# A chain of eight layers on one core: signs turned, forget rows as matmuls, whole first units, a new table of modulation sums

## The chip, the cores and the metric

The kernel runs on one core of a Trainium2 chip. The metric is the device time of one execution in microseconds (us), lower is better. It is one program for the whole chain.

## The reference

Eight stages follow one another on x of 256 x 1024 (float32): moba attention with pooling, a gated feed-forward with a causal convolution (conv), and then twice a plain ffn, an attention mixer and a second plain ffn; the mixer is swa (window 128, sinks, relative bias) the first time and fox (forget gates) the second.

```python
mod = c_act @ ada_w[l] + ada_b[l]              # shift, scale, gate of every stage
h = rms_norm(x, norm1_g[l]) * (1 + scale1) + shift1
...
def swiglu(h, w13, w2):
    gate, up = jnp.split(h @ w13, 2, axis=-1)
    return (jax.nn.silu(gate) * up) @ w2
...
# swa: m = max(max(s), sink); p = exp(s - m); denom = sum(p) + exp(sink - m)
s = jnp.einsum('bqhgd,bkhd->bhgqk', qb, kb).astype(jnp.float32) + bias
...
# fox: F is the running sum of log_sigmoid(fl + b_f)
s = jnp.einsum('bqhd,bkhd->bhqk', qb, k).astype(jnp.float32)
s = s + Fq[..., None] - F[:, :, None, :]
p = jax.nn.softmax(s, axis=-1)
...
x = x + 0.5 * mod[:, 0, 2][:, None, :] * swiglu(h, ffn_w13[layer, 0], ffn_w2[layer, 0])
```

## The kernel before

**Units of weights.** All weights stream once through SBUF in 215 units of 2048 columns on 128 partitions. SyncE loads a unit into `raw` (a ring of five); ACT copies it to `hi` in a rounded format (line 487); DVE writes `lo` = raw − hi (line 915, in `split_to`). PE then multiplies with three matmuls for each product: hi·hi, hi·lo and lo·hi (`product`). The next raw load into a slot of the ring waits for `unit_done` of the unit five earlier. The stages are moba (units 0 to 23), conv (24 to 56), ffn (57 to 89), swa (90 to 99), ffn (100 to 132), ffn (133 to 165), fox (166 to 181) and ffn (182 to 214); in what follows they are stages 0 to 7, and a unit is counted from its stage's start.

**An ffn stage.** Eleven slices j of 256 hidden columns. Units (j, 0) and (j, 1) hold the slice's gate and up weights, each for half of the contraction; both are multiplied for tile 0 and then for tile 1 of the tokens. Unit (j, 2) holds the down weights. From slice 2 on the order is (j, 0), (j, 1), (j−1, 2): units 3j−1, 3j, 3j+1. On ACT, in `ffn_step`, stand the hi split of unit 3j+1, the silu of tile 0, the silu of tile 1 (line 580), which waits for `unit_done` of unit 3j, and behind it the hi split of unit 3j+2. On DVE the lo split of unit 3j+1, the two products of silu and up (line 998), the lo split of unit 3j+2, and the low part of the hidden (line 1008) stand in this order, with the pieces and columns that go with each lo split.

**Modulation.** The vector of shifts, scales and gates is computed in chunks of 512 outputs, six a stage. The weights of a chunk come in four pieces over POOL's queue. DVE multiplies a piece by c and adds it to `ada_sum` (`pieces`, lines 874 and 877); the first piece of chunk c waits for `ada_used`, the sum of chunk c−2. PE adds up over the partitions with four matmuls of one column (`sums`, line 1392), and waits there for the columns of all chunks before (`mod_ready`). DVE adds the bias and writes the column (`columns`, line 899). `gate_rows` (line 1404) turns a stage's gate columns to rows on PE, into the same bank M as the sums; it waits until the columns of all sums issued so far are written, and the next user of M waits for ACT's copy (`gate_copy`, line 546). The dictionaries `PIECES_AT`, `SUMS_AT`, `COLS_AT`, `GATES_AT`, computed at the head of the file, say at which unit each of these stands: on PE a sum or a gate turn comes ahead of the unit's matmuls (`take`); on DVE pieces and then columns come behind the unit's lo split. `CHUNKS_IN` says how many chunks fall in a stage. By the table before, stage 2 (nine chunks) has sums at units 7, 10, 13, 16, 19 and so on, columns at 9, 12, 15, 18 and gate turns at 13 and 16; stages 4 and 5 (eight chunks) have sums at 7, 10, 14, 17, 21, columns at 9, 12, 16, 19 and gate turns at 13 and 17.

**Start of a stage.** x is normalised on ACT (line 515), transposed on PE (`turn_x`, line 1412), scaled out of the banks on ACT (line 527), and split on DVE into `h_hi` and `h_lo` (lines 950 and 952), for two tiles of 128 tokens, in halves. In stages 0 and 1 `first_units` (line 1321 and on) runs units 0 and 1 for tile 0 alone with 128-column matmuls, and then for tile 1.

**Attention.** A head's logits are two matmuls (lines 1609 and 1610); DVE adds the bias and takes the maximum (lines 1081 and 1082), negates it (1085), in swa adds the sink (1089); ACT exponentiates (657, 658); PE transposes and multiplies by V. In fox DVE first forms the bias of the head from the forget rows in TB, Fq and the mask (1071 and 1073), and POOL fetches these rows: it writes them to DRAM (456) and reads them to all partitions (459). The steps t = 0 to 19 overlap the heads, and carry the remaining rows of the in-projection (`step_rows`), lo splits, pieces and out pieces (`step_out`); at the end of the steps stand out pieces (3,0), (1,1), (2,1), the transposes of the next stage's tile 0 and (3,1).

## Time and profile before

| | before |
|---|---|
| times of three runs, us | 1655.14, 3947.6, 1659.46 (the median) |
| profiled execution, us | 1657.64 |
| its span, us | 1655.8 |
| mean granted TensorE clock | 0.933 |
| PE busy, us (share) | 1518.7 (92%) |
| DVE busy | 1075.1 (65%) |
| ACT busy | 725.3 (44%) |
| POOL busy | 135.4 (8%) |
| DMA, mean | 203 GB/s |

The span is that of the profiled execution from its first to its last instruction; times in the rows are microseconds from its start. PE is the TensorE matmul queue, PEld its weight loads. A granted clock of 1.00 is 2.4 GHz and 0.50 is 1.2 GHz. A row of a timeline gives start, duration, engine, line, operation, what is written from what, and in brackets the idle time of the engine before it and what ended that.

### The profile page before, as it was taken

What the parts mean: (1) busy time and instruction counts of PE and PEld (TensorE: products, weight loads), DVE (VectorE), ACT (ScalarE), POOL (GpSimd) and SP (SyncE); (2) the same over time, 40 slices, a digit from 0 to 9 for tenths busy, and PEclk for the clock granted to TensorE, in tenths of its full rate; (3) what the DMA queues carried; (4) which work ended last, traced back from release to release, by engine and by line L of the source; (5) the groups of instructions that cost most, each with busy time, mean ns of one, the idle gap of its engine ahead of it and who ended that gap; (6) DMA issues with size and microseconds to landing.
All of it is one profiled execution on the core that took longest, in us unless ns stands there. A gap on an engine that the chain in (4) does not pass through costs nothing.

```text
span 1655.8 us, 19732 instructions
## 1 busy us (share of the span) xinstructions
PE 1518.7 (92%) x7897; PEld 1282.6 (77%) x7897; DVE 1075.1 (65%) x1571; ACT 725.3 (44%) x1030; POOL 135.4 (8%) x195
## 2 busy tenths in 40 slices
PE   1898898999998999998799999999999987999998
PEld 1897897988887777886467888878888765678886
DVE  4226776478787666775856767677676467666454
ACT  3224443444446433354546334553445555563442
POOL 1000110010110111100100111001110000000000
PEclk9569899799999999999689999999999897899999
DMA  9325676377684887863417888678886354067562
GB/s 320 116 90 175 201 247 204 115 228 242 216 260 135 263 270 241 294 224 143 140 52 224 291 278 274 206 227 290 273 270 210 126 204 152 26 204 237 174 196 80
DMA packets 194990, 335.97 MB, mean 203 GB/s; under 512 B 8338, under 2 KB 138030, under 8 KB 194772
## 3 DMA queue, kind: packets, MB, share of 16 engines
q1 hardware_dynamic: 167536, 236.02, 42.3%
q0 software_dynamic: 26784, 98.47, 18.7%
q8 instruction: 63, 1.03, 0.3%
q10 hardware_dynamic: 580, 0.23, 0.1%
q14 instruction: 27, 0.22, 0.0%
HBM read 333.58 MB, written 1.10 MB: 202 GB/s over the span
## 4 chain that ended last, share of the span: by engine, by line
PE 73%; DVE 12%; ACT 7%; issue 4%; DMA 3%; SPq 0%; ACTq 0%; DVEq 0%
PE bank L1461 9%; PE bank L1463 9%; PE bank L1462 9%; PE bank L1424 7%; PE bank L1426 6%; PE bank L1425 6%; PE bank L1321 5%; PE bank L1322 5%; PE bank L1323 5%; DVE lo L915 3%; ACT hi L487 3%; DVE ada_sum L877 3%; PE bank L1392 2%; PE bank L1472 1%; DMA ada<-in_ada_w 1%
## 5 line engine op out<-in xcount | busy, mean ns | idle before, releaser
L915 DVE TENSOR_TENSOR lo<-raw,hi 128x2048 fp32r<-128x2048 f32 x215 | 490.9, 2287 | 102.2 <-ACT hi L487 101.7
L487 ACT ACTIVATE hi<-raw 128x2048 fp32r<-128x2048 f32 x215 | 405.4, 1909 | 32.6 <-DMA raw<-in_w_out 19.3
L1461 PE MATMUL bank<-hi,h_hi 128*128 128x512 f32 x704 | 277.6, 394 | 2.6 <-DVE lo L915 1.8
L1463 PE MATMUL bank<-hi,h_lo 128*128 128x512 f32 x704 | 274.4, 390 | 0.0
L1462 PE MATMUL bank<-lo,h_hi 128*128 128x512 f32 x704 | 274.1, 389 | 0.0
L877 DVE SCALAR_TENSOR_TENSOR ada_sum<-ada,c_act,ada_sum 128x512 f32<-128x512 f32 x308 | 231.1, 750 | 34.4 <-DMA ada<-in_ada_w 26.4
L1424 PE MATMUL bank<-hi,o_hi 128*128 128x512 f32 x504 | 209.4, 415 | 18.5 <-DVE lo L915 16.4
L449 POOL DMA_DIRECT2D ada<-in_ada_w x176 | 125.5, 713 | 1230.4 <-DVE ada_sum L877 1202.6
L1321 PE MATMUL bank<-h_hi,hi 128*128 128x256 f32 (+1 forms) x640 | 196.7, 307 | 17.1 <-DVE lo L915 10.9
L1426 PE MATMUL bank<-hi,o_lo 128*128 128x512 f32 x504 | 202.1, 401 | 0.0
L1425 PE MATMUL bank<-lo,o_hi 128*128 128x512 f32 x504 | 201.5, 400 | 0.0
L1322 PE MATMUL bank<-h_lo,hi 128*128 128x256 f32 (+1 forms) x640 | 194.1, 303 | 0.0
L1323 PE MATMUL bank<-h_hi,lo 128*128 128x256 f32 (+1 forms) x640 | 194.1, 303 | 0.0
L580 ACT ACTIVATE KT<-bank 128x256 f32<-128x256 f32 x88 | 33.8, 384 | 324.4 <-PE bank L1463 323.9
L1461 PEld LDWEIGHTS bank<-hi,h_hi 128*128 128x128 f32 x704 | 132.2, 188 | 32.5 <-DVE lo L915 3.5
L1463 PEld LDWEIGHTS bank<-hi,h_lo 128*128 128x128 f32 x704 | 132.2, 188 | 28.3
L1321 PEld LDWEIGHTS bank<-h_hi,hi 128*128 128x128 f32 x640 | 137.2, 214 | 20.2 <-issue 15.7
L1462 PEld LDWEIGHTS bank<-lo,h_hi 128*128 128x128 f32 x704 | 132.3, 188 | 26.4
L1322 PEld LDWEIGHTS bank<-h_lo,hi 128*128 128x128 f32 x640 | 137.2, 214 | 0.0
L1323 PEld LDWEIGHTS bank<-h_hi,lo 128*128 128x128 f32 x640 | 137.0, 214 | 0.0
L1424 PEld LDWEIGHTS bank<-hi,o_hi 128*128 128x128 f32 x504 | 97.9, 194 | 41.3 <-DVE lo L915 20.7
L998 DVE TENSOR_TENSOR KT<-KT,bank 128x256 f32<-128x256 f32 x88 | 36.5, 420 | 125.8 <-ACT KT L580 125.8
(209 smaller groups left out, 1884.3 us busy)
## 6 DMA issues: line engine op xcount, KB each, us to landing
ada<-in_ada_w POOLq DMA_DIRECT2D x176, 512.0 KB, 4.9
raw<-in_ffn_w SPq DMA_DIRECT2D x176, 512.0 KB, 5.2
raw<-in_ffn_w SPq DMA_DIRECT2D x44, 1024.0 KB, 6.0
raw<-in_w_up SPq DMA_DIRECT2D x22, 1024.0 KB, 5.1
raw<-in_w_in SPq DMA_DIRECT2D x16, 1024.0 KB, 6.9
raw<-in_fox_w_in SPq DMA_DIRECT2D x12, 1024.0 KB, 5.2
raw<-in_w_down SPq DMA_DIRECT2D x11, 1024.0 KB, 5.3
raw<-in_swa_w_in SPq DMA_DIRECT2D x6, 1024.0 KB, 5.2
```

Of the source, the lines that this page charges most:

```text
L487: nc.scalar.activation(hi[:, n % NS, :], raw[:, n % NS, :], ACT.Copy).then_inc(hi_ready, 1)
L877: nc.vector.scalar_tensor_tensor(acc, in0=src, scalar=c_act[:, col:col + 1], in1=acc, op0=ALU.mult, op1=ALU.add).then_inc(ada_step, 1)
L915: nc.vector.tensor_tensor(lo[:, n % NS, :], raw[:, n % NS, :], hi[:, n % NS, :].bitcast(F32), ALU.subtract).then_inc(lo_ready, 1)
L1321: mm(outp, wh, xh, start=start, stop=False, skip_group_check=True)
L1322: mm(outp, wh, xl, start=False, stop=False, skip_group_check=True)
L1323: return mm(outp, wl, xh, start=False, stop=stop, skip_group_check=True)
L1424: mm(outp, xk_hi, wh[:, k, cut], start=start, stop=False, skip_group_check=True)
L1425: mm(outp, xk_hi, wl[:, k, cut], start=False, stop=False, skip_group_check=True)
L1426: ins = mm(outp, xk_lo, wh[:, k, cut], start=False, stop=stop, skip_group_check=True)
L1461: mm(bank[:, :], xk_hi, wh[:, i, :], start=k == 0, stop=False, skip_group_check=True)
L1462: mm(bank[:, :], xk_hi, wl[:, i, :], start=False, stop=False, skip_group_check=True)
L1463: ins = mm(bank[:, :], xk_lo, wh[:, i, :], start=False, stop=k == KD - 1, skip_group_check=True)
```

## The change

Seven things change together. (1) Stages 0 and 1 run their first two units whole, on both tiles with 256-column matmuls (`whole_units`); in conv the transposes of tile 1 stand ahead of them. (2) `CHUNKS_IN` gives stages 4 and 5 nine chunks and fox none, and the table puts a sum two units later where a gate turn stands at its unit, its column two units behind it: stages 2, 4 and 5 have sums at 7, 10, 15, 18, 19, 22, 25, 28, 31, columns at 9, 12, 17, 20, 21, 24 and gate turns at 13 and 16. (3) Logits are kept negated: DVE writes the negative minimum directly, and the two small operations (1085, 1089) go; the exponential takes a scale of −1. (4) In fox the forget terms become two extra matmuls of K = 2 for each head; TB is filled with ones on POOL, two rows a head are written by four small transfers, and lines 1071 and 1073, the copy of Fq and its transposes go. (5) The in-projection in fox uses three banks in turn, and more of its rows come ahead of the steps in swa (12 instead of 8 of 16 of the last two blocks) and fewer in fox. (6) Out pieces (1,1) and (2,1) stand in steps 15 and 18. (7) In swa two pieces stand ahead of the steps, and eight in them; block roots, evictions and splits of ACT and DVE are placed in other steps.

```diff
-ROWS_STEP = {"swa": 2, "fox": 6}
-ROWS_LEFT = {"swa": 8, "fox": 40}
+ROWS_FROM = {"swa": 12, "fox": 16}
+ROWS_STEP = {"swa": 2, "fox": 7}
...
-CHUNKS_IN = [6, 6, 9, 3, 8, 8, 2, 2]
+CHUNKS_IN = [6, 6, 9, 3, 9, 9, 0, 2]
...
-        for c0 in range(n0):
-            SUMS_AT[w0 + at[4 * c0 + 3] + 2] = 1
-            COLS_AT[w0 + min(at[4 * c0 + 3] + 4, 32)] = 1
-        free = [u0 for u0 in range(at[7] + 5, 33) if not any(0 < u0 - at[4 * c0 + 3] - 2 <= 2 for c0 in range(n0))]
-        GATES_AT[w0 + free[0]] = (s0, 0)
-        GATES_AT[w0 + next(u0 for u0 in free if u0 >= free[0] + 2)] = (s0, 1)
+        due = [at[4 * c0 + 3] + 2 for c0 in range(n0)]
+        free = [u0 for u0 in range(at[7] + 5, 33) if not any(0 < u0 - u1 <= 2 for u1 in due)]
+        turns = (free[0], next(u0 for u0 in free if u0 >= free[0] + 2))
+        GATES_AT[w0 + turns[0]], GATES_AT[w0 + turns[1]] = (s0, 0), (s0, 1)
+        for u1 in due:
+            u1 += 2 * (u1 in turns)
+            SUMS_AT[w0 + u1] = 1
+            COLS_AT[w0 + min(u1 + 2, 32)] = 1
...
-PIECES_STEP = {"moba": (), "swa": range(0, 10), "fox": range(2, 8)}
-SUMS_STEP = {"moba": (), "swa": (2, 6, 10), "fox": (4, 8)}
-COLS_STEP = {"moba": (), "swa": (3, 7, 10), "fox": (5, 9)}
+PIECES_STEP = {"moba": (), "swa": range(0, 8), "fox": ()}
+SUMS_STEP = {"moba": (), "swa": (1, 5, 9), "fox": ()}
+COLS_STEP = {"moba": (), "swa": (2, 6, 10), "fox": ()}
...
+                pool.wait_ge(am_done, HEAD0[6])
+                nc.gpsimd.memset(TB[0:66, :, :], 1.0).then_inc(rows_ones, 1)
+                pool.wait_ge(rows_ones, 1)
                 pool.wait_ge(nft_ready, 1)
-                pool.dma_start(scratch_f[:, :], nFT).then_inc(forget_out, 16)
+                pool.dma_start(scratch_f.rearrange("n h t -> h n t"), F_rows).then_inc(forget_out, 16)
                 pool.wait_ge(forget_out, 16)
...
-                pool.dma_start(TB[:, :, :].rearrange("p a b -> p (a b)"), src).then_inc(bias_in, 16)
-            last_before_forget = PIECES * sum(CHUNKS_IN[:6]) + 1
+                for odd in range(2):
+                    for n in range(2):
+                        pool.dma_start(TB[64 * odd + 1 - n:64 * odd + 2 - n, 8 - 8 * n:16 - 8 * n, :],
+                                       scratch_f[n:n + 1, odd:16:2, :]).then_inc(bias_in, 16)
...
-                nc.scalar.activation(pr[:, 0:P], pr[:, 0:P], ACT.Exp, bias=st[:, 2:3], accum_out=st[:, 4:5])
-                ins = nc.scalar.activation(pr[:, P:384], pr[:, P:384], ACT.Exp, bias=st[:, 3:4], accum_out=st[:, 5:6])
+                nc.scalar.activation(pr[:, 0:P], pr[:, 0:P], ACT.Exp, bias=st[:, 2:3], scale=-1.0, accum_out=st[:, 4:5])
+                ins = nc.scalar.activation(pr[:, P:384], pr[:, P:384], ACT.Exp, bias=st[:, 3:4], scale=-1.0,
+                                           accum_out=st[:, 5:6])
                 if KINDS[s] == "swa":
-                    ins = nc.scalar.activation(st[:, 6:8], st[:, 6:8], ACT.Exp)
+                    ins = nc.scalar.activation(st[:, 6:8], st[:, 2:4], ACT.Exp, bias=sink[:, h:h + 1])
...
-                b0, b1 = TB[:, h, P:2 * P], TB[:, h, :]
-                if kind == "fox":
...
-                    nc.vector.scalar_tensor_tensor(f0, in0=TB[:, h, 0:P], scalar=Fq[:, 0, h:h + 1], in1=mask[:, P:2 * P],
-                                                   op0=ALU.add, op1=ALU.add)
-                    nc.vector.scalar_tensor_tensor(f1, in0=TB[:, h, :], scalar=Fq[:, 1, h:h + 1], in1=mask,
-                                                   op0=ALU.add, op1=ALU.add).then_inc(bias_ready, 1)
-                    b0, b1 = f0, f1
-                    dve.wait_ge(bias_ready, h + 1)
...
+                b0, b1 = (mask[:, P:2 * P], mask) if kind == "fox" else (TB[:, h, P:2 * P], TB[:, h, :])
+                most = nsink[:, h:h + 1] if kind == "swa" else -LOWEST
                 dve.wait_ge(qk_done, n + 1)
                 if n >= 3:
                     dve.wait_ge(tr_done, n - 2)
-                nc.vector.tensor_tensor_reduce(pr[:, 0:P], L[:, 0:P], b0, 1.0, least, ALU.add, ALU.max, st[:, 0:1])
-                nc.vector.tensor_tensor_reduce(pr[:, P:384], L[:, P:384], b1, 1.0, least, ALU.add, ALU.max,
-                                               st[:, 1:2]).then_inc(max_done, 1)
-                dve.wait_ge(max_done, n + 1)
-                ins = nc.vector.tensor_scalar(st[:, 2:4], st[:, 0:2], -1.0, None, ALU.mult)
-                if kind == "swa":
-                    ins.then_inc(neg_done, 1)
-                    dve.wait_ge(neg_done, h + 1)
-                    ins = nc.vector.tensor_scalar(st[:, 6:8], st[:, 2:4], sink[:, h:h + 1], None, ALU.add)
-                ins.then_inc(am_done, 1)
+                nc.vector.tensor_tensor_reduce(pr[:, 0:P], L[:, 0:P], b0, -1.0, most, ALU.add, ALU.min, st[:, 2:3])
+                nc.vector.tensor_tensor_reduce(pr[:, P:384], L[:, P:384], b1, -1.0, most, ALU.add, ALU.min,
+                                               st[:, 3:4]).then_inc(am_done, 1)
...
+                    pieces(2)
...
-                        if t in (0, 4):
-                            block_sums(s, 4 + t // 4)
-                            block_norm(s, 4 + t // 4)
-                        if t in (1, 3, 5, 7, 9):
-                            split_through(s, 6 + (t - 1) // 2)
+                        if t in (0, 3):
+                            block_sums(s, 4 + t // 3)
+                            block_norm(s, 4 + t // 3)
+                        if t in (2, 4, 6, 8, 10):
+                            split_through(s, 6 + (t - 2) // 2)
...
+                    dve.wait_ge(cum_done, 1)
+                    nc.vector.tensor_copy(F_rows[:, 0, :], A[1][0:16, 0:T])
+                    nc.vector.tensor_scalar(F_rows[:, 1, :], A[1][0:16, 0:T], -1.0, None, ALU.mult).then_inc(nft_ready, 1)
...
-            def first_units(s):
-                for t in range(2):
-                    for u in range(2):
-                        w, bank = W0[s] + u, G[u]
-                        if t == 0:
-                            take(w)
-                        wh, wl = unit_of(w, KD)
+            def whole_units(s):
+                if s:
+                    turn_x(s, 1)
+                for u in range(2):
+                    w, bank = W0[s] + u, G[u]
+                    take(w)
+                    wh, wl = unit_of(w, KD)
+                    for n in range(2):
                         for k in range(KD):
-                            pe.wait_ge(h_ready, 4 * s + 2 * t + k // 4 + 1)
-                            xk_hi, xk_lo = h_hi[:, k, P * t:P * (t + 1)], h_lo[:, k, P * t:P * (t + 1)]
...
-                            for n in range(2):
-                                ins = product(bank[:, T * n + P * t:T * n + P * (t + 1)], wh[:, k, P * n:P * (n + 1)],
-                                              wl[:, k, P * n:P * (n + 1)], xk_hi, xk_lo, k == 0 and n == 0, k == KD - 1)
-                        if t:
-                            ins.then_inc(unit_done, 1)
-                    if t == 0 and s:
-                        turn_x(s, 1)
+                            if u == 0 and n == 0:
+                                pe.wait_ge(h_ready, 4 * s + 3 + k // 4)
+                            ins = product(bank[:, T * n:T * (n + 1)], wh[:, k, P * n:P * (n + 1)],
+                                          wl[:, k, P * n:P * (n + 1)], h_hi[:, k, :], h_lo[:, k, :], k == 0, k == KD - 1)
+                    ins.then_inc(unit_done, 1)
...
+                if KINDS[s] != "fox":
+                    mm(L[:, 0:P], q[:, 0:P], k[:, 0:P], start=True, stop=True)
+                    mm(L[:, P:384], q[:, P:T], k, start=True, stop=True).then_inc(qk_done, 1)
+                    return
+                f_q, f_k = TB[row:row + 2, 8 + h // 2, :], TB[row:row + 2, h // 2, :]
+                mm(L[:, 0:P], q[:, 0:P], k[:, 0:P], start=True, stop=False, skip_group_check=True)
+                mm(L[:, 0:P], f_q[:, 0:P], f_k[:, 0:P], start=False, stop=True, skip_group_check=True)
+                mm(L[:, P:384], q[:, P:T], k, start=False, stop=False, skip_group_check=True)
+                mm(L[:, P:384], f_q[:, P:T], f_k, start=False, stop=True, skip_group_check=True).then_inc(qk_done, 1)
...
                     elif t == 14:
                         step_out(s, 0, 1)
+                    elif t == 15:
+                        step_out(s, 1, 1)
                     elif t == 17:
                         step_out(s, 2, 0)
                     if t >= 3:
                         values(s, t - 3)
+                    if t == 18:
+                        step_out(s, 2, 1)
                 step_out(s, 3, 0)
-                step_out(s, 1, 1)
-                step_out(s, 2, 1)
                 turn_x(s + 1, 0)
...
-                    block_rows(s, 3, 0, 0, KD)
-                    pe.wait_ge(nft_ready, 1)
-                    steps(s, (1, 3, 4, 6))
+                    pe.wait_ge(bias_in, 96)
+                    steps(s, (3, 4, 5, 6))
```

**Order 1.** DVE in stage 2, from the last piece behind unit 15's lo split on. Line 915 is the lo split of unit 16, then of unit 17; 877 are pieces, 899 is a column. Before:

```order
L877 SCALAR_TENSOR_TENSOR ada_sum<-ada,c_act,ada_sum 128x512 [waits ada_step]
L899 TENSOR_TENSOR modc<-bank,cols 128x4 [waits ada_used]
L915 TENSOR_TENSOR lo<-raw,hi 128x2048 [waits hi_ready]
L877 SCALAR_TENSOR_TENSOR ada_sum<-ada,c_act,ada_sum 128x512 [waits ada_step,ada_full0]
L877 SCALAR_TENSOR_TENSOR ada_sum<-ada,c_act,ada_sum 128x512 [waits ada_step]
L998 TENSOR_TENSOR KT<-KT,bank 128x256 [waits silu_ready] x2
L915 TENSOR_TENSOR lo<-raw,hi 128x2048 [waits hi_ready]
```

After, the same splits are line 923, the pieces 885, the column 907:

```order
L885 SCALAR_TENSOR_TENSOR ada_sum<-ada,c_act,ada_sum 128x512 [waits ada_step]
L923 TENSOR_TENSOR lo<-raw,hi 128x2048 [waits hi_ready]
L885 SCALAR_TENSOR_TENSOR ada_sum<-ada,c_act,ada_sum 128x512 [waits ada_step,ada_full0]
L885 SCALAR_TENSOR_TENSOR ada_sum<-ada,c_act,ada_sum 128x512 [waits ada_step]
L1006 TENSOR_TENSOR KT<-KT,bank 128x256 [waits silu_ready] x2
L923 TENSOR_TENSOR lo<-raw,hi 128x2048 [waits hi_ready]
L885 SCALAR_TENSOR_TENSOR ada_sum<-ada,c_act,ada_sum 128x512 [waits ada_step,ada_full1]
L885 SCALAR_TENSOR_TENSOR ada_sum<-ada,c_act,ada_sum 128x512 [waits ada_step]
L907 TENSOR_TENSOR modc<-bank,cols 128x4 [waits ada_used]
L1016 TENSOR_TENSOR o_lo<-bank,o_hi 128x512 [waits hid_hi_done]
```

The column of the last sum moved from ahead of unit 16's lo split to behind unit 17's lo split and its piece.

**Order 2.** PE in stage 2, at the end of unit 15 (slice 5, second half). Before, both the gate turn (line 1404) and the sum (line 1392) stand ahead of unit 16's first matmul (line 1424):

```order
L1462 MATMUL bank5<-lo,h_hi 128x512
L1463 MATMUL bank5<-hi,h_lo 128x512
L1404 MATMUL bank6<-kon,modc 128x128 [waits gate_ready,mod_ready]
L1404 MATMUL bank6<-kon,modc 128x128 x3
L1392 MATMUL bank6<-ones,ada_sum 128x1 [waits gate_ready,mod_ready,ada_step]
L1392 MATMUL bank6<-ones,ada_sum 128x1 x3
L1424 MATMUL bank0<-hi,o_hi 128x512 [waits hid_ready,lo_ready]
```

After, the sum (line 1371) stands ahead of unit 15's first matmul:

```order
L1440 MATMUL bank5<-hi,h_hi 128x512
L1441 MATMUL bank5<-lo,h_hi 128x512
L1442 MATMUL bank5<-hi,h_lo 128x512
L1371 MATMUL bank6<-ones,ada_sum 128x1 [waits gate_ready,mod_ready,ada_step]
L1371 MATMUL bank6<-ones,ada_sum 128x1 x3
L1440 MATMUL bank4<-hi,h_hi 128x512 [waits lo_ready]
```

And at the end of unit 15 the gate turn (line 1383) stands alone ahead of unit 16:

```order
L1441 MATMUL bank5<-lo,h_hi 128x512
L1442 MATMUL bank5<-hi,h_lo 128x512
L1383 MATMUL bank6<-kon,modc 128x128 [waits gate_ready,mod_ready]
L1383 MATMUL bank6<-kon,modc 128x128 x3
L1403 MATMUL bank0<-hi,o_hi 128x512 [waits hid_ready,lo_ready]
```

The gate turn now follows a sum that was issued one unit before it, and the next sum (line 1371) stands ahead of unit 18.

**Order 3.** PE in fox, the first logits. Before:

```order
L1575 MATMUL bank5<-lo,h_hi 128x512
L1576 MATMUL bank5<-hi,h_lo 128x512
L1609 MATMUL bank0<-KT,QT 128x128 [waits am_done,bk_ready]
L1610 MATMUL bank0<-KT,QT 128x256
L1609 MATMUL bank1<-KT,QT 128x128 [waits am_done]
```

After, with the forget matmuls from TB (lines 1599 and 1601):

```order
L1558 MATMUL bank6<-hi,h_lo 128x512
L1598 MATMUL bank0<-KT,QT 128x128 [waits am_done,bk_ready]
L1599 MATMUL bank0<-TB 128x128
L1600 MATMUL bank0<-KT,QT 128x256
L1601 MATMUL bank0<-TB 128x256
L1598 MATMUL bank1<-KT,QT 128x128 [waits am_done]
```

Each head has four matmuls where it had two.

## Rows read from the trace of the kernel before

**Rows 1.** Cores: span and mean granted clock

```profile
core 0: 1655.8 us, clock 0.933
```

**Rows 2.** Windows, core 0 (engines' busy us, PEclk, DMA share, GB/s): stages 2, 4; swa's, fox's steps

```profile
525.00:737.30 212.30, 204.56 (x939) 168.59 (x937) 150.50 (x167) 90.63 (x103) 25.65 (x36) 0.97 0.76 251
872.00:1073.90 201.90, 197.40 (x932) 163.01 (x931) 144.19 (x158) 90.78 (x103) 22.81 (x32) 1.00 0.77 255
...
780.20:835.20 55.00, 39.88 (x145) 25.99 (x146) 47.68 (x134) 29.69 (x74) 7.12 (x10) 0.67 0.42 130
1345.80:1413.20 67.40, 56.73 (x230) 40.45 (x230) 47.92 (x130) 38.15 (x75) 4.28 (x6) 0.82 0.41 136
```

**Rows 3.** Windows of first units: stage 0 (two), conv (two), and 256-column matmuls in conv

```profile
63.00:104.00 41.00, 41.00 (x193) 41.00 (x193) 7.79 (x9) 9.04 (x13) 0.00 (x0) 0.50 0.12 38
104.20:109.00 4.80, 4.80 (x24) 4.80 (x24) 2.36 (x2) 2.56 (x3) 0.00 (x0) 0.50 0.72 219
291.60:302.20 10.60, 10.60 (x97) 10.60 (x97) 9.37 (x11) 6.78 (x10) 0.14 (x1) 1.00 0.40 137
305.70:325.90 20.20, 20.20 (x100) 20.20 (x101) 2.77 (x6) 3.68 (x7) 0.00 (x0) 0.53 0.17 53
423.10:434.50 11.40, 11.40 (x97) 11.40 (x97) 8.07 (x10) 3.38 (x4) 1.43 (x2) 1.00 0.72 239
```

**Rows 4.** Timeline of DVE, stage 0, tile 1's first half

```profile
64.95 0.69 DVE L952 TENSOR_TENSOR h_lo<-tn,h_hi 128x512 fp32r<-128x512 f32 x1
```

**Rows 5.** Windows where PE's clock has fallen and comes back

```profile
264.60:269.40 4.80, 4.77 (x15) 4.19 (x16) 4.38 (x2) 2.40 (x2) 2.56 (x3) 0.50 0.54 167
512.00:515.00 3.00, 2.99 (x7) 2.41 (x8) 2.97 (x4) 2.77 (x3) 0.00 (x0) 0.50 0.00 0
515.00:518.00 3.00, 3.00 (x14) 2.40 (x14) 1.64 (x2) 0.00 (x0) 0.00 (x0) 0.97 0.00 0
```

**Rows 6.** Timeline of ACT, conv's start: tile 1's scaling

```profile
298.16 1.32 ACT L515 ACTIVATE work<-x,rms 128x512 f32<-128x512 f32 x2
```

**Rows 7.** Timeline of ACT, stage 5, behind unit 15

```profile
1177.10 0.38 ACT L580 ACTIVATE KT<-bank 128x256 f32<-128x256 f32 x1 [2.34 <-PE bank L1463]
```

**Rows 8.** Timeline of DVE, stage 5, unit 17's split and piece

```profile
1179.33 2.29 DVE L915 TENSOR_TENSOR lo<-raw,hi 128x2048 fp32r<-128x2048 f32 x1 [1.39 <-ACT hi L487]
1181.54 1.53 DVE L877 SCALAR_TENSOR_TENSOR ada_sum<-ada,c_act,ada_sum 128x512 f32<-128x512 f32 x2
```

**Rows 9.** Timeline of PE, stage 2, the sum at unit 13

```profile
611.90 1.02 PE L1392 MATMUL bank<-ones,ada_sum 128*128 128x1 f32 x8 [1.96 <-ACT gate L546]
```

**Rows 10.** Timeline of DVE in swa's steps

```profile
808.04 0.17 DVE L1085 TENSOR_SCALAR stat<-stat 128x2 f32<-128x2 f32 x1
808.24 0.23 DVE L1089 TENSOR_SCALAR stat<-stat,sink 128x2 f32<-128x2 f32 x1
...
811.79 2.29 DVE L915 TENSOR_TENSOR lo<-raw,hi 128x2048 fp32r<-128x2048 f32 x1 [0.70 <-ACT hi L487]
```

**Rows 11.** Timeline of ACT in swa's steps, a table load and the next exponential

```profile
806.32 1.28 ACT L657 ACT_TABLE_LOAD   x1
808.51 0.40 ACT L657 ACTIVATE work<-work,stat 128x128 f32<-128x128 f32 x1 [0.90 <-DVE stat L1089]
```

**Rows 12.** Timeline of PE, swa's end, the start of out piece (3,0)

```profile
863.36 0.47 PE L1424 MATMUL bank<-hi,o_hi 128*128 128x512 f32 x1 [1.07 <-DVE o_lo L1107]
```

**Rows 13.** Timeline of ACT, swa's end: tile 0 normalised for the next stage

```profile
869.16 1.34 ACT L515 ACTIVATE work<-x,rms 128x512 f32<-128x512 f32 x2 [0.23 <-DVE rms L943]
```

**Rows 14.** Timeline of DVE in fox, the first bias

```profile
1344.15 0.35 DVE L1071 SCALAR_TENSOR_TENSOR tn<-TB,Fq,kon 128x128 f32<-128x128 f32 x1 [3.16 <-DMA TB<-forget_rows]
```

**Rows 15.** Groups of PE by shape, whole span: the logits

```profile
L1610 PE MATMUL bank<-KT,QT 64*128 64x256 f32 x80 | 26.4, 436 | 0.0
L1609 PE MATMUL bank<-KT,QT 64*128 64x128 f32 x80 | 20.7, 361 | 18.8 <-DVE stat L1085 6.6 <-DVE stat L1089 5.9 <-issue 2.9
```

**Rows 16.** Timeline of POOL in fox: the broadcast of the forget rows

```profile
1335.30 0.58 POOL L459 DMA_DIRECT2D TB<-forget_rows  x1 [4.28 <-DMA forget_rows<-tn]
```

More of the change, by code:

```diff
@@ L265, in bank_of, with product_bank @@
             return (G[0], G[1], A[2], A[3])[u % 4] if u in QK_UNITS[KINDS[s]] else G[u % 2]
-        def product_bank(b, t):
-            return A[2 + b] if t and b < 2 else G[b] if b < 2 else G[t]
+        def product_bank(s, b, t):
+            if b < 2:
+                return A[2 + b] if t else G[b]
+            return (G[0], G[1], M)[(2 * (b - 2) + t) % 3] if KINDS[s] == "fox" else G[t]
         def logit_bank(h):
@@ L473, in _ @@
             by_distance(1, 16)
+            load_pieces(6)
+            forget_rows()
             load_pieces(NST)
@@ L1591, in step_rows @@
             def step_rows(s, t):
[L1593 to L1596 removed]
+                kind = KINDS[s]
+                first = ROWS_FROM[kind] + ROWS_STEP[kind] * t
+                for r in range(first, min(first + ROWS_STEP[kind], 2 * KD * (len(BLOCKS[kind]) - 2))):
+                    n = r // KD
+                    block_rows(s, 2 + n // 2, n % 2, r % KD, r % KD + 1)
             def logits(s, h):
```

169 lines of the change are left out of this document (72 added, 97 removed).

## The prediction

> **What bounds the kernel now.** First the span and the clock: 1655.8 us at a mean granted TensorE clock of 0.933 [rows 1]. Then the windows by stage [rows 2]: in a plain ffn stage PE is busy 197.4 of 201.9 us at clock 1.00, with DVE at 144 and ACT at 91. There every idle microsecond of PE is a microsecond of the end. In the swa steps it is otherwise: of 55.0 us DVE is busy 47.7 and PE 39.9 at 0.67, so DVE sets the pace. The windows of the first units [rows 3] show PE fully busy but at clock 0.50 and on 128-column matmuls, which are dear by the column. So I price PE in ffn stages by waits, in the steps by DVE's work, and in the first units by count and clock.
>
> **Whole first units, stage 0.** Before, 192 matmuls of 128 columns take 41 us at 0.50, 0.213 each [rows 3], and end at about 104.2. They begin as soon as tile 0 is split. Now 96 matmuls of 256 columns begin when tile 1's first h_lo is there: 64.95 + 0.69 = 65.6 [rows 4]. The same form at half clock takes 4.80/24 = 0.20 each, and on the full clock 11.40/97 = 0.118 [rows 3]. If all stay at half clock it is 19.2 us, to 84.9, a gain of 19. If the clock comes back after some 5 us, as it does elsewhere [rows 5], it is 24 × 0.20 + 72 × 0.12 = 13.4, to 79.1, a gain of 25. I take −25, since steady work got the clock back within 5 us where the stretches show it return [rows 5]; bound −19, and 0 by a rival below. The chain to unit 2's splits has been idle long before, so nothing new is late.
>
> **Whole first units, conv.** Before, tile 0's half (97 matmuls, 10.6 us at 1.00) ran under tile 1's normalising, and tile 1's half took 20.2 us at 0.53, to 325.9 [rows 3]. Now nothing runs until tile 1 is there: its scaling on ACT ends at 299.5 [rows 6], then transposes, the four scalings out of the banks, a cast and an h_lo of 0.69, with pieces between on DVE: about 303.0. With 13.4 us behind it, 316.4, a gain of 9.5. At half clock throughout (19.2), 322.2, a gain of 3.7. Clock 0.53 in the old second half says that idle costs it here too; I keep the 13.4. One sum moved away from a gate turn at unit 17 is 0.8 more.
>
> The isolated back-to-back gap that the Trainium skill ("TensorE: Matmul & The Clock Gate", section "Back-to-back issue gap") gives, N/1.2 cold and N/2.4 + 2.5 ns warm, prices by columns. By it, whole units save nothing, and only the later start would be left. The rows speak against it: 97 matmuls of half the width took 10.6 us and 97 of the full width 11.4, both at 1.00 [rows 3]; the same section says that the formula under-counts for small N.
>
> **The table of sums, columns and gates in ffn stages.** This is the largest term. Stages 2, 4 and 5 now have nine chunks each, with sums at units 15, 18, 19 and gate turns at 13 and 16. A gate turn (gate_rows) waits for the columns (mod_ready) of all sums issued so far. At unit 16 that includes the sum of unit 15, whose column DVE now writes only behind the lo split of unit 17 and its piece. Likewise the sum at unit 19 waits for the column of unit 18's sum, which stands behind lo of unit 20. PE executes in order, so everything of unit 16 is queued behind that wait. And lo(17) cannot be early: its hi on ACT stands behind the silu of tile 1, and that waits for unit 15's last matmul. From stage 5: the silu starts at 1177.10 when PE's last matmul releases it [rows 7]; hi follows it on ACT and releases lo at 1179.33; lo runs to 1181.6 and the piece to 1183.07 [rows 8]; the column adds some 0.15. PE was done at about 1176.9. The wait is 6.3 us; a blocked piece on DVE (chunk c waits for the sum of c−2) adds up to 0.9. I take 6.8 a wait, six waits: 40.8 (38 to 43). The clock then falls: behind an idle the rows show 3 to 5 us at 0.50 before 0.97 [rows 5], so half of that, 1.5 to 2.4, is lost; 2.0 × 6 = 12. Against it, stage 2 already pays for nine chunks and for two collisions of sum and gate (1.96 us for the copy of the gate [rows 9]): 212.3 against 201.9 of stage 4 [rows 2], less 0.8 for its additional sum, leaves 9.6 that go. Stages 4 and 5 lose 0.8 each by one more sum and win 0.8 each by a gate and a sum that no longer meet. Four more pieces each on DVE are 3.1 us, under PE. Sum: 40.8 + 12 − 9.6 = +43.2 (37 to 55).
>
> **Swa.** DVE sets the pace. The two small stat operations (0.17 and 0.23 [rows 10], with gaps about 0.42) leave each head; ten heads in the pace-setting part give −4.2. Two pieces of 1.53 leave the steps [rows 8]: −3.1. The waits of lo for hi, 0.70 [rows 10], go in five steps, since ACT's hi is now a step ahead: −3.5. The block root in step 0 adds two table loads of 1.28 on ACT [rows 11]: +2.6. Together −8.2. The Trainium skill ("ScalarE: Activation LUTs", section "What ACT_TABLE_LOAD costs") adds a drain of about 1.38 us to each switch; by it the −8.2 would be −5.4. The load ends at 807.60, and the exponential behind it starts at 808.51 after 0.90 idle that DVE ended [rows 11], so a drain does not show, though it could lie in that idle. At the tail: two out pieces of 12 matmuls, half a unit each (a unit is 197.4/33 = 6.0 with its small matmuls [rows 2], 5.6 without, so 5.6 for both), ran behind piece (3,0) and covered tile 0's normalising. Moved to t = 15 and 18 they meet few gaps: 1.07 before (3,0) [rows 12] and one half as long, 1.6. So (3,0) starts 4.0 later. Normalised rows are there at 869.16 + 1.34 = 870.5 [rows 13], 7.1 behind the start of (3,0), where before the transposes came 8.3 behind: −1.2, up to −1.8. PE idles in between, clock +1.5. Tail +4. Swa: −4 (−9 to +2).
>
> **Fox.** Per head two DVE operations (the first 0.35 [rows 14]) become two K = 2 matmuls on PE. The forms nearest by shape take 0.361 and 0.436 [rows 15], 0.88 a head with a gap: 16 × 0.88 = +14 on PE. Seven block rows move from ahead of the steps into them: 7 × 3 matmuls at 0.23 = +4.8. The two sums there go: −1.6. Together 17.2 more work in the steps, in which PE waits 67.4 − 56.7 = 10.7 us at a clock of 0.82 [rows 2]: the waits take 10.7 of it, and a denser PE gets back perhaps 4 of the clock. That leaves +2.5. The start: before, POOL issued the broadcast of 2 MB at 1335.3 [rows 16], and DVE had it at 1344.15 after waiting 3.16 [rows 14]. Now four small transfers land by about 1335, and PE, with fewer rows ahead of the steps, idles some 5.6 for them, then starts the logits at about 1341, 1.3 earlier than before. The moved out pieces and a thinner cover at the end cost 4, as in swa. Total +5; if the waits take all and the clock recovers −5, if they take half +14.
>
> **Sum.** −25 − 10.3 + 43.2 − 4 + 5 = +8.9 on the profiled execution's own 1657.6 us: 1666.5. That execution lies between the other two usable times, 1655.1 and 1659.5 (the median), so I do not shift it: **1666**. About 2% is what a measurement of this kernel can tell from no change, 1626 and 1693.
>
> **Rivals.**
> *The columns come in time.* If the six waits don't show (DVE or ACT ahead of what stage 5's rows show, or my reading of the table is off by a chunk), the ffn term is −9.6 and the result about 1614. For it: only the order shows the wait. Against: the waits name the very semaphores, and silu, hi and lo stand in that order [rows 7, 8].
> *The clock stays at half between the waits.* The waits at 16 and 19 are three units apart: 3/33 of 197.4 us [rows 2], 17.2 without the small matmuls, at full clock. If the clock doesn't come back there, this stretch becomes 34, three times: +51, less 3 × 2.0 already counted: about 1712, slower. It decides where a wait costs more than 6.4 us of clock in place of 2.0. For: 41 us of busy 128-column work stayed at 0.50 [rows 3]. Against: 512-column work got back to 0.97 within 3 us [rows 5].
> *Whole units give nothing*, because PE's time goes by columns: stage 0 then ends 2.7 later by its later start, conv 1 earlier (303.0 + 10.6 + 11.4), 36 above the forecast: 1703, slower. For: in stage 0 PE shows no idle at all. Against: 0.213 a matmul of 128 columns and 0.20 of 256 at the same half clock [rows 3].
> *Fox waits longer*: the fill of TB and five small transfers arrive as late as the old broadcast, and the K = 2 matmuls find no gaps: fox +20, about 1681.
>
> **How the numbers follow.** Forecast 0.70 (its own range 1643 to 1691), columns in time 0.13, clock at half 0.07, whole units nothing 0.02, fox longer 0.08. The range leaves out the first and the third rival: 1638 to 1694. Faster is the first rival and a tail, 0.14; slower the second and third and a tail, 0.11; the rest 0.75.
>
> **What would show it.** In the changed profile: stage 0's first units end near 79 to 85; in stages 2, 4 and 5 the gate matmul at unit 16 and the sum at unit 19 each show an idle of 6 to 7 us released by DVE's column, and each stage takes 215 to 222 us; swa's steps are shorter by about 8 us, its tail longer; fox's first logits near 1341 less the shift. Idles of under 2 us at these two places would make the forecast wrong by 40 us; a granted clock of 0.50 across whole units between them would make it too low.

## The result

| | before | after |
|---|---|---|
| median, us (18 runs each) | 1656.82 | 1668.51 |
| profiled execution's span, us | 1655.8 | 1669.1 |
| mean granted clock | 0.933 | 0.945 |

The ratio of after to before is 1.0064, with a 95% interval of 1.0048 to 1.008: slower by 0.6%, clear of noise and well inside 2%. One run of each kernel took over twice as long and is no part of the ratio. The prediction was 1666, in a range of 1638 to 1694.

The change in time by stage, each counted from the first transposes for it (their weight load) to those for the next, from the two traces:

| stage | before | after | difference | forecast |
|---|---|---|---|---|
| 0, moba | 287.7 | 261.0 | −26.7 | −25 |
| 1, conv | 236.6 | 225.9 | −10.7 | −10.3 |
| 2, 4, 5, ffn | 618.8 | 662.8 | +44.0 | +43.2 |
| 3, swa | 134.4 | 133.6 | −0.8 | −4 |
| 6, fox | 175.5 | 180.6 | +5.1 | +5 |
| 7, ffn | 203.0 | 205.3 | +2.3 | 0 |

So a kernel that moved by 12 us holds a gain of 37 and a loss of 44. The windows of after by stage (ffn 2, 4 and 5; columns as in [rows 2]):

```profile
486.90:706.60 219.70, 203.38 (x942) 167.75 (x941) 149.63 (x167) 90.76 (x103) 25.65 (x36) 0.96 0.74 244
...
840.10:1061.00 220.90, 205.44 (x939) 170.17 (x940) 151.31 (x168) 91.37 (x104) 25.66 (x36) 0.95 0.71 234
1061.00:1283.20 222.20, 205.66 (x941) 169.37 (x941) 150.54 (x170) 90.75 (x103) 27.78 (x35) 0.95 0.72 237
```

In stage 4, PE is now idle for 15 us where it was idle for 4.5, with the clock at 0.95 in place of 1.00: both a wait and what the wait does to the clock.

The timeline of PE in stage 2 of after, at the gate turn of unit 16 and the sum of unit 19:

```profile
594.87 2.08 PE L1383 MATMUL bank<-kon,modc 128*128 128x128 f32 x8 [6.18 <-DVE modc L907]
...
621.50 1.84 PE L1371 MATMUL bank<-ones,ada_sum 128*128 128x1 f32 x8 [6.32 <-DVE ada_sum L885]
```

The six such waits in the three stages are 6.18, 6.32, 6.12, 6.21, 6.12 and 6.59 us, 37.5 together. The rows of DVE ahead of the first of them tell why:

```profile
583.19 0.49 DVE L882 TENSOR_SCALAR ada_sum<-ada,c_act 128x512 f32<-128x512 f32 x1 [4.33 <-PE bank L1371]
...
591.01 2.28 DVE L923 TENSOR_TENSOR lo<-raw,hi 128x2048 fp32r<-128x2048 f32 x1
593.21 1.53 DVE L885 SCALAR_TENSOR_TENSOR ada_sum<-ada,c_act,ada_sum 128x512 f32<-128x512 f32 x2
594.66 0.15 DVE L907 TENSOR_TENSOR modc<-bank,cols 128x4 f32<-128x4 f32 x1
```

The column (line 907) stands behind the lo split of unit 17 (the row at 591.01) and its pieces; it ends at 594.81, and the gate matmul starts at 594.87. The row of the second wait names a piece (line 885) as its releaser, but a column of the same kind ended at 621.40 and PE's weight load began at 621.48, so there too it is the column. The first row is a piece that was held up: DVE waited 4.33 us for the sum that the table had moved.

The first units, after (windows; stage 0 from 70.2 on, and conv), answer to [rows 3]:

```profile
70.20:79.10 8.90, 8.90 (x69) 8.90 (x69) 2.33 (x2) 2.40 (x2) 0.00 (x0) 1.00 0.34 105
276.40:290.00 13.60, 13.60 (x100) 13.60 (x101) 2.70 (x6) 3.12 (x5) 0.00 (x0) 0.86 0.38 117
```

Of stage 0's 96 whole matmuls the first starts at 65.93 and the last at 80.09, where before the first units ended near 104. In conv the first starts 15.3 us behind the stage's start and the last 28.5; the forecast had 15.3 and 28.7 for start and end.

### The profile page after: what moved, and what is told of

It reads as the page before. It is cut to its first block, busy times and chain, and to the rows that moved or that the text cites. A ratio compares the mean times of both kernels' runs of the same rounds, so it can differ in the third digit from the quotient of the medians.

```text
span 1669.1 us, 19395 instructions
## 1 busy us (share of the span) xinstructions
PE 1507.7 (90%) x7767; PEld 1256.2 (75%) x7767; DVE 1054.2 (63%) x1484; ACT 733.3 (44%) x1034; POOL 140.5 (8%) x199
## 4 chain that ended last, share of the span: by engine, by line
PE 75%; DVE 13%; ACT 5%; DMA 4%; issue 3%; SPq 0%; ACTq 0%; POOL 0%; DVEq 0%; POOLq 0%
PE bank L1440 8%; PE bank L1442 8%; PE bank L1441 8%; PE bank L1403 7%; PE bank L1404 6%; PE bank L1405 6%; PE bank L1307 4%; PE bank L1309 4%; PE bank L1308 4%; DVE lo L923 4%; DVE ada_sum L885 4%; DMA ada<-in_ada_w 3%; PE bank L1371 2%; ACT hi L493 2%; PE bank L1556 2%
## 5 line engine op out<-in xcount | busy, mean ns | idle before, releaser
L1403 PE MATMUL bank<-hi,o_hi 128*128 128x512 f32 x504 | 213.8, 424 | 16.4 <-DVE lo L923 16.4
L1307 PE MATMUL bank<-h_hi,hi 128*128 128x256 f32 x576 | 167.7, 291 | 19.3 <-DVE lo L923 10.6
L1308 PE MATMUL bank<-h_lo,hi 128*128 128x256 f32 x576 | 165.0, 287 | 0.0
L1309 PE MATMUL bank<-h_hi,lo 128*128 128x256 f32 x576 | 164.9, 286 | 0.0
L1403 PEld LDWEIGHTS bank<-hi,o_hi 128*128 128x128 f32 x504 | 100.2, 199 | 39.5 <-DVE lo L923 20.7
L1307 PEld LDWEIGHTS bank<-h_hi,hi 128*128 128x128 f32 x576 | 112.8, 196 | 22.6 <-issue 20.1
L1405 PEld LDWEIGHTS bank<-hi,o_lo 128*128 128x128 f32 x504 | 99.4, 197 | 22.9
L1404 PEld LDWEIGHTS bank<-lo,o_hi 128*128 128x128 f32 x504 | 100.0, 198 | 18.5
L1308 PEld LDWEIGHTS bank<-h_lo,hi 128*128 128x128 f32 x576 | 112.9, 196 | 0.0
```

What stands on the lines that cost most here:

```text
L1307: mm(outp, wh, xh, start=start, stop=False, skip_group_check=True)
L1308: mm(outp, wh, xl, start=False, stop=False, skip_group_check=True)
L1309: return mm(outp, wl, xh, start=False, stop=stop, skip_group_check=True)
L1403: mm(outp, xk_hi, wh[:, k, cut], start=start, stop=False, skip_group_check=True)
L1404: mm(outp, xk_hi, wl[:, k, cut], start=False, stop=False, skip_group_check=True)
L1405: ins = mm(outp, xk_lo, wh[:, k, cut], start=False, stop=stop, skip_group_check=True)
```

## The experiments

All are compared with the kernel before on the same chip. Stage times are from each run's trace.

**The column one unit sooner.** The changed kernel with

```diff
+            moved = u1 in turns
-            u1 += 2 * (u1 in turns)
+            u1 += 2 * moved
             SUMS_AT[w0 + u1] = 1
-            COLS_AT[w0 + min(u1 + 2, 32)] = 1
+            COLS_AT[w0 + min(u1 + 2 - (moved and kind0 == "ffn"), 32)] = 1
```

> The changed kernel with one edit: in plain ffn stages the column of a moved sum stands one unit behind the sum, not two (units 16 and 19 in place of 17 and 20). My theory (PE waits at units 16 and 19 for a column that stands behind a late lo split): all six waits of 6.1 to 6.6 us go, and the clock lost behind them, so stages 2, 4 and 5 fall from about 221 to 203 to 206 us each, in all 45 to 50 us less than the changed kernel, some 1620 us. Rival (the stages are longer because nine chunks of pieces load DVE and DMA more): the waits move to the next sum or to lo splits, and at least half of the 44 us stays, above 1640 us.

Median 1630.9, ratio to before 0.9871 (0.9818 to 0.9925); the profiled span is 1622.3. Stages 2, 4 and 5 took 209.6, 208.4 and 208.1 where after has 219.7, 220.9 and 222.2: 36.7 of the 44 are gone. They did not reach the 203 to 206 of my theory, since the waits did not vanish but shrank to between 1.84 and 2.02. The rival, the load of nine chunks, had at least half of the 44 staying; 7.3 stayed. What was left needed a cause. The timelines of PE and, ahead of it, DVE in stage 2 of this run:

```profile
588.13 1.80 PE L1384 MATMUL bank<-kon,modc 128*128 128x128 f32 x8 [1.89 <-DVE modc L908]
```

```profile
580.75 0.49 DVE L883 TENSOR_SCALAR ada_sum<-ada,c_act 128x512 f32<-128x512 f32 x1 [4.33 <-PE bank L1372]
...
586.46 1.54 DVE L886 SCALAR_TENSOR_TENSOR ada_sum<-ada,c_act,ada_sum 128x512 f32<-128x512 f32 x2 [0.60 <-DMA ada<-in_ada_w]
587.92 0.15 DVE L908 TENSOR_TENSOR modc<-bank,cols 128x4 f32<-128x4 f32 x1
```

The piece waits 4.33 us for the sum of two chunks before, which stands two units later than its pieces allow. All that follows on DVE, the column too, is late by that.

**One of the two.** The same edit for the first moved sum alone (column at unit 16, the other still at unit 20):

```diff
+            moved = u1 in turns
+            first = moved and u1 == turns[0]
-            u1 += 2 * (u1 in turns)
+            u1 += 2 * moved
...
-            COLS_AT[w0 + min(u1 + 2, 32)] = 1
+            COLS_AT[w0 + min(u1 + 2 - (first and kind0 == "ffn"), 32)] = 1
```

> The changed kernel with the earlier column for the first moved sum alone (column at unit 16; that of unit 18's sum stays at unit 20). My theory, with each wait costing itself and about 2 us of clock: the wait at unit 16 goes, the one at 19 stays, half of the gain of the earlier columns, 22 to 25 us less than the changed kernel, some 1645 us. Rival (the clock is lost once for both waits, since they are three units apart): the one wait left costs over 8.5 us a stage and the gain is less than 19 us, above 1650 us.

Median 1647.75, ratio 0.9958 (0.9934 to 0.9981), span 1645.8. The trace shows the waits at unit 16 at 1.70 to 1.94 and those at unit 19 still at 6.17 to 6.26. The three stages took 216.7, 214.2 and 217.2, together 648.1: between 662.8 with both long waits and 626.1 with both shortened. One kind gave 14.7 and the other 22.0, of which 12.9 and 12.7 are idle time (three times 4.3); the rest, 1.8 and 9.3, is clock. By the ratios the steps are 18 and then 14 us. This does not decide between theory and rival. The median lies below the rival's 1650, but a gain of 14.7 by stages, or 18 by ratios, lies below the rival's 19 and short of my 22 to 25. Each kind of wait costs clock of its own (the granted clock of the three stages is 0.95 to 0.96 in after, 0.97 here and 0.98 to 0.99 with both columns early), but not the same 2 us: the second kind costs more.

**The old rule for sums beside gate turns**, nine chunks kept:

```diff
-            u1 += 2 * (u1 in turns)
+            u1 += 2 * (u1 in turns and kind0 == "conv")
```

> The changed kernel with the old rule in plain ffn stages: sums at units 13 and 16 beside the gate turns, nine chunks kept. My theory: two waits of about 2 us for the copy of the gate in each of three stages in place of 6.3, so each of these stages takes what stage 2 of the kernel before took, about 212 to 213 us; 24 us less than the changed kernel, some 1645 us. Rival (a wait costs no clock when it is only 2 us long): 208 to 209 us a stage, some 1632 us.

Median 1630.9, ratio 0.9843 (0.9793 to 0.9894), span 1637.7. The stages took 211.3, 211.0 and 210.5, in each two waits of 1.96 for the gate's copy, as in [rows 9]. By the traces that is 30 us less than after (37 by the ratios); a stage lies between my 212.5 and the rival's 208.5, and the median is nearer to the rival's 1632 than to my 1645. Its "no clock" does not hold all the same: the three stages take 632.8, against 607.5 with the table of the run "gate turns between the sums" below, so six waits of 1.96 us cost 25.3, of which 11.8 are waiting. And the new rule, which avoids 1.96 us, brings 6.2.

**Whole first units alone.** The kernel before with `first_units` replaced by `whole_units` in stages 0 and 1.

```diff
...
-                first_units(s)
+                whole_units(s)
...
```

> The kernel before with whole first units in stages 0 and 1 and nothing else changed. My theory: stage 0 is 25 to 27 us shorter and conv 9 to 10, together 35 us less than the kernel before, about 1622 us. Rival (part of conv's gain came from the sum that left unit 17, or the start of stage 0 gained by something else in the change): under 30 us.

Median 1618.0, ratio 0.9794 (0.9753 to 0.9835): 34 us by the ratio. By stage −25.4 in moba and −8.6 in conv. The 2 us more that after gains in conv (225.9 against 228.0) go with the table there, where a sum left unit 17. No run tries this alone, but the waits of PE in the two traces are alike within 0.1 us up to that unit; there this run waits 0.78 for the gate's copy and 1.62 at its next long wait, where after has 0.64 and 0.72. This part of the change alone gives everything that the change gains.

**Gate turns between the sums.** The changed kernel with

```diff
+        if kind0 == "ffn" and n0 == 9:
+            turns = (15, 18)
+            for u1 in due:
+                SUMS_AT[w0 + u1] = 1
+                COLS_AT[w0 + min(u1 + (1 if u1 + 2 in turns else 2), 32)] = 1
+            GATES_AT[w0 + turns[0]], GATES_AT[w0 + turns[1]] = (s0, 0), (s0, 1)
+            continue
```

> The changed kernel with another table in plain ffn stages with nine chunks: sums stay at units 13 and 16, their columns stand one unit behind them (14, 17), and the gate turns stand between sums, at 15 and 18. In the run with earlier columns 1.9 us of each wait stayed, since the first piece of a chunk waits for the sum of two chunks before, and that sum had been moved two units later. My theory: with no sum moved, neither the column nor the copy of the gate is waited for, the gaps of 1.9 us go, and stages 2, 4 and 5 take 203 to 205 us each, some 12 to 15 us less than with earlier columns: 1608 to 1618 us. Rival (the copy of the gate on ACT now stands ahead of the hi split of units 16 and 19 and delays it): gaps of 1 to 3 us behind lo splits, 208 us or more a stage, no gain over 1630 us.

Median 1611.8, ratio 0.9733 (0.9694 to 0.9773), span 1602.4. Stages 2 and 4 in the windows of this run; stage 5 took 202.1:

```profile
485.10:688.00 202.90, 198.51 (x942) 164.11 (x941) 149.57 (x167) 91.00 (x103) 25.64 (x36) 1.00 0.80 264
...
821.40:1023.90 202.50, 199.40 (x939) 165.58 (x940) 151.04 (x168) 91.47 (x104) 25.64 (x36) 0.99 0.77 256
```

PE has the same 942 instructions as in after's stage 2, in 202.9 us in place of 219.7. No wait over 1.2 us is left in them but one of 2.07 at each stage's first down unit, which before has too. So nine chunks cost nothing themselves, and the table's two waits a stage with their clock cost 16.8, 18.4 and 20.1 us, 55.3 in all: 37.5 of waiting and 17.8 of clock. (Against the kernel before it is 44, since stage 2 there already paid 10.)

**The same table in the kernel before**, with whole first units and everything else as before. The diff is the one above, put into the kernel of whole first units alone; it acts on stage 2 only, since the other ffn stages have eight chunks there.

> The kernel before with whole first units and the gate turns between the sums in stage 2, the one stage with nine chunks there; signs, forget rows, banks and out pieces as before. My theory: stage 2 falls from 212 to 204 us, so 8 us less than whole first units alone, about 1610 us; against the changed kernel with the same table this tells what signs, forget rows, banks and moved out pieces are worth together: by the two traces' swa and fox stages -1 and between -5 and +5 us. Rival (the rest of the change is worth some per cent that the table hides): the changed kernel with this table is faster by over 15 us.

Median 1610.7, ratio 0.9721 (0.9692 to 0.9749), span 1609.4, stage 2 at 202.1. It stands level with the changed kernel with that table (0.9733). The two intervals overlap almost wholly: signs, forget rows as matmuls, three banks and moved out pieces together are worth nothing that shows in the times. By the traces swa is 135.7 here and 133.5 there, and fox 171.1 in both.

**Out pieces back** behind (3,0), on the run with gate turns between the sums:

```diff
-                    elif t == 15:
-                        step_out(s, 1, 1)
...
-                    if t == 18:
-                        step_out(s, 2, 1)
                 step_out(s, 3, 0)
+                step_out(s, 1, 1)
+                step_out(s, 2, 1)
```

> The run with the gate turns between the sums, and the two moved out pieces of tile 1 back behind piece (3,0) in swa and fox. My theory: piece (3,0) starts some 5 us earlier, the transposes of the next stage 1.5 us later behind it, and PE no longer waits 3.6 us for the normalised rows, so the next stage also gets back 2.4 us of clock; the pieces' own 5.6 us come back there: 1 to 4 us less for each of the two stages, 2 to 8 us in all. Rival (moving them filled gaps that now open again): equal or slower.

Median 1599.4, ratio 0.9674 (0.9627 to 0.9721), the fastest of all runs that keep the forget gates. Swa 133.5 → 131.5, fox 171.1 → 168.9, stage 7 205.3 → 204.5: 5 us by stage. The intervals of the two ratios overlap, and stage times alone scatter as much (stage 5, whose code is the same, was 2.3 longer in this profile). The sign rests on the tail: from the last maximum to the next stage's transposes it takes 21.8 us, in swa and in fox, in all six traces with the moved pieces, and 19.7 to 19.8 in all six without. The steps ahead of it gained nothing by the move: swa's last maximum comes 111.4 us behind the stage's start with the pieces moved and 111.6 with them back. PE at the end of swa, in after and then in this run, shows what the pieces cover:

```profile
840.14 1.97 PE L1391 MATMUL bank<-kon,work 128*128 128x128 f32 x8 [3.59 <-ACT work L521]
```

```profile
819.63 1.03 PE L1398 MATMUL bank<-kon,work 128*128 128x128 f32 x8
```

The wait for the normalised rows is gone, and the eight transposes take 1.03 us in place of 1.97.

**Without forget matmuls.** On the run with gate turns between the sums, fox's 32 matmuls of K = 2, two a head, are left out, so that fox attends without forget gates.

```diff
...
-                mm(L[:, 0:P], f_q[:, 0:P], f_k[:, 0:P], start=False, stop=True, skip_group_check=True)
...
-                mm(L[:, P:384], f_q[:, P:T], f_k, start=False, stop=True, skip_group_check=True).then_inc(qk_done, 1)
```

> The run with the gate turns between the sums, without the forget matmuls: the 32 matmuls of K = 2 that add the forget terms are left out, so fox attends without its forget gates. My theory (a small K does not make a matmul cheap: 0.4 us each at the going clock, partly in gaps): fox is 6 to 12 us shorter. Rival (K = 2 costs next to nothing, or all of it lies in gaps): under 3 us.

Median 1583.0, ratio 0.9562 (0.9533 to 0.9591). Fox fell from 171.1 to 152.3, by 18.8, more than my 6 to 12. The medians differ by 29, with four runs each; what of that lies outside fox is scatter or not shown, since the code of the other stages is the same (in this profile stage 5 was 5.6 longer and swa 2.2 shorter). The groups of PE by shape, of the run that keeps them:

```profile
L1608 PE MATMUL bank<-TB 2*128 2x256 f32 x32 | 12.1, 461 | 0.0
L1607 PE MATMUL bank<-KT,QT 64*128 64x256 f32 x32 | 11.7, 446 | 0.0
L1605 PE MATMUL bank<-KT,QT 64*128 64x128 f32 x32 | 8.0, 333 | 1.1 <-issue 1.1
L1606 PE MATMUL bank<-TB 2*128 2x128 f32 x32 | 8.0, 332 | 0.0
```

The trace has two records for each of these f32 matmuls (32 for 16 heads), and records overlap, so a price is read from the busy time: (12.1 + 8.0)/16 = 1.26 a head. The rows ahead of the prediction say the same, (26.4 + 20.7)/40 heads = 1.18 [rows 15], and 18.8/16 = 1.18. I had added the mean durations of one record each, 0.8. Nor does a part lie in gaps: this kernel's fox has 8 us of gaps in all, of which 1.1 in the heads' steps.

**Block root ahead again**, on the run with out pieces back:

```diff
+                    block_root(s, 4)
                     for t in range(HEADS[kind] + 3):
                         attention_step(s, t)
-                        if t == 0:
-                            block_root(s, 4)
-                        elif t == 1:
+                        if t == 1:
```

> The run with gate turns between the sums and the out pieces back, and in swa ACT's block root of block 4 ahead of the steps again, where the kernel before had it. The prediction priced its place in step 0 at two table loads of 1.28 us in DVE's pace. My theory: swa falls from 131.5 to 129 us. Rival (ACT's loads lie in its own slack, and the root ahead makes the first exponential wait for DVE's sums of step 0): no gain, or 1 to 3 us longer.

Swa 131.5 → 130.2, half of what I expected and not the rival's loss. From the first maximum to head 11's it took 48.3 us, where the seven traces with the root in step 0 and the signs turned lie between 49.0 and 49.3, so about 1 us of it is clear. Median 1609.45, ratio 0.973 (0.9692 to 0.9768), above the run it is built on. By stages, fox took 178.3 in its profile against 168.9, with the same code, and stage 2 207.0 against 202.5; this edit does not touch either stage, and the section on the hardware shows such differences with the code the same.

**Two small DVE operations a head added again** in swa, on the same run; their result is unused.

```diff
...
+                    nc.vector.tensor_scalar(st[:, 0:2], st[:, 2:4], -1.0, None, ALU.mult).then_inc(neg_done, 1)
+                    dve.wait_ge(neg_done, h + 1)
+                    ins = nc.vector.tensor_scalar(st[:, 0:2], st[:, 0:2], sink[:, h:h + 1], None, ALU.add)
```

> The run with gate turns between the sums and the out pieces back, and in swa two small DVE operations on 128x2 per head added behind the second maximum, each waiting for the one before as in the kernel before; their result is not used. My theory (DVE sets the pace of heads 0 to 11, 0.42 us a head): from the first maximum to that of head 11 the steps grow from 49.3 by 4 to 5 us, swa from 131.5 to 136. Rival (other waits set the pace since the change): under 1.5 us.

From the first maximum to head 11's took 51.9 in place of 49.2, so +2.7, and swa went from 131.5 to 133.9: between my 4 to 5 and the rival's 1.5. Median 1612.6, ratio 0.9736 (0.9692 to 0.9781). The signs save about 0.25 us a head, not 0.42 (which is argued from this one pair of traces): DVE sets the pace only part of the time.

## Why the prediction was right

By the two traces the stages add up to +13.3 against the forecast +8.9. The two large terms came out by their mechanism; part of the closeness is luck, as the paragraphs on fox and on the table say.

*Whole first units.* −26.7 and −10.7 against −25 and −10.3. The start in conv came within 0.1 us, by adding up one chain, and the price by matmul (0.20, 0.12) held: the matmuls come 0.21 us apart for the first 4 us in conv and 6 us in stage 0, and 0.12 after. In stage 0 the difference of 1.7 is no more than scatter, since the same code took 258.6 to 262.1 there in the other runs. In conv two errors cancel: whole units alone gave 8.6 where I had 9.5, and the sum that left unit 17 goes with 2.1 where I had 0.8. Whole units alone give 34 us in a kernel of their own, and the rival of a price by columns is gone.

*The table.* +44.0 against +43.2, but with three errors that cancel. The waits were 6.26 on average in place of 6.8 (−3.2 over six), since the piece that was held up did not add to them: the hi split behind the silu ended at 590.90, DVE was through with what that piece had delayed at 591.1, and lo began at 591.01. The chain silu, hi, lo, piece, column alone gives the 6.3 of the prediction. The clock cost more, 17.8 in place of 12 (+5.8): 3.0 a wait. The term "1.5 to 2.4 of clock a wait" was the mis-sized one. And what the old tables already cost was 11.3 (55.3 less 44.0) in place of 9.6 (−1.7). The mechanism, two waits a stage for a column behind a late split, is shown by the rows and by two tables that take it away. The rival with the clock at half from unit 16 to 19 did not come about: in after's stage 2 the clock was back 3 us behind the first wait. Behind the second it stayed at half for more than 6 us:

```profile
595.00:598.00 3.00, 3.00 (x12) 2.76 (x13) 0.00 (x0) 0.60 (x1) 0.72 (x1) 0.55 0.69 204
598.00:601.00 3.00, 3.00 (x17) 2.47 (x16) 0.00 (x0) 0.38 (x1) 0.00 (x0) 1.00 0.18 74
...
621.60:624.60 3.00, 3.00 (x11) 2.74 (x12) 0.00 (x0) 0.00 (x0) 0.72 (x1) 0.50 0.79 245
624.60:627.60 3.00, 3.00 (x8) 2.31 (x7) 0.00 (x0) 0.00 (x0) 0.00 (x0) 0.50 0.18 71
627.60:630.60 3.00, 3.00 (x15) 2.38 (x14) 0.69 (x1) 1.50 (x2) 0.00 (x0) 0.86 0.00 0
```

Stages 4 and 5 show the same. By such windows of after, the time lost to the clock (a window's length times one less its clock) is 1.4 to 2.2 us behind a first wait and 3.4 to 3.9 behind a second, an estimate of 16.5 of the 17.8. So the price taken from [rows 5] fitted the first kind of wait and not the second. Why the clock comes back later behind the second stays open.

*Swa.* −0.8 against −4. The steps from head 0 to head 11 fell from 57.1 to 49.2, −7.9 against my −8.2, though not in the parts given: the signs are worth 2.7 of the 4.2, the table loads 1.3 of the 2.6. (In the two runs with gate turns between the sums, swa is 133.5 against 135.7, so −2.2.) What I missed is ahead: four more block rows stand before the first logits, and the first maximum came 3.3 us later (46.4 behind the stage's start, before 43.1). I had named the rows moved into and out of the steps for fox and not priced them for swa. The tail came near: +3.8 against +4. Piece (3,0) started 127.1 behind the stage's start, before 126.3, and the wait for the normalised rows is 3.59. Of the 3.8, 2.0 go with the moved pieces.

*Fox.* +5.1 against +5, and this one is luck. The same stage took 171.1 in the runs where the clock held, for the changed code and for the code of before alike, so its true term is near 0 and the 5 are a state of the clock. In parts: the first maximum came 4.1 us earlier than in the profile of before, but that is mostly clock too, for in two other profiles the code of before has it at 62.9 and 63.0 us behind the stage's start. The changed code has it between 61.3 and 63.2, so at its lowest 1.6 earlier (forecast 1.3). The forget matmuls took 18.8 (forecast 14, from mean durations where the busy time was to be read), and the gaps in the whole stage went from 20 us to 8.

*Stage 7* (+2.3, forecast 0): it starts behind the wait of 3.58 that the moved out pieces left, and at a lower clock. The term "PE idles in between, clock +1.5" belongs to the stage that follows. With the pieces back it still takes 204.5, so that explains 0.8 of the 2.3; the kernel before with whole units and the new table took 204.5 with stage 7's code unchanged. The rest may be the clock's scatter; no run settles it.

## What to carry to other kernels

Where a wait asks for "all issued so far" (here the gate turn, for the columns of all sums), moving one sum later holds up every such wait behind it. Look first where the slowest link stands (here a lo split that waits for a silu), then leave the sum where it is and move the gate turn, which has slack. A table that avoided a wait of 2 us brought waits of 6 us, and the cure was to put the gate turn where no sum is pending, with the column ahead of it one unit sooner. A change that sums to nothing may hold a gain and a loss of 40 us each: take the stages apart and keep the part that pays.

## What the runs showed of the hardware

The same code at the same place runs at one or the other clock for 20 us, with PE shown as busy throughout. The windows of 20 us from about 120 us behind fox's start, of after and then of the run with gate turns between the sums:

```profile
1403.00:1423.00 20.00, 20.00 (x53) 11.33 (x53) 12.16 (x32) 10.36 (x20) 0.00 (x0) 0.51 0.04 12
```

```profile
1346.00:1366.00 20.00, 20.00 (x90) 12.22 (x91) 15.12 (x41) 15.03 (x32) 0.00 (x0) 1.00 0.01 4
```

53 matmuls in one and 90 in the other. With the changed kernel's fox the stage took 180.6 in two profiles (after and the old rule) and 171.1 to 172.9 in three; with the code of before 175.5 in one and 171.1 in two. With the out pieces back it took 168.9, 178.3 and 176.4, though the edits between these three lie in swa. Ffn stages scatter too: stage 5 took 207.6 in the run without forget matmuls and 202.1 with the same code for that stage, stage 2 took 207.0 in one run and 202.5 in another. Single times of after reach from 1659.8 to 1672.8, a scatter of this size. A term of under 10 us in such a stage can't be read from one profile of each kernel. What decides which clock it gets stays open.

A matmul with K = 2 costs as much as one with K = 64: busy 12.1 and 8.0 us against 11.7 and 8.0 for the same count and columns, in the run with gate turns between the sums; leaving the 32 out made fox 18.8 us shorter.
